# Four slots of split weights, each moved to a different byte offset within 512 bytes

## The reference

```python
proj = jnp.einsum('btd,de->bte', h, w_in[l])            # first block, 2 layers
x = x + jnp.einsum('btd,de->bte', merged, w_out[l])
gu = jnp.einsum('btd,df->btf', h2, w_gate_up[l])
x = x + jnp.einsum('btf,fd->btd', jax.nn.silu(g) * up, w_down[l])
...
proj = h @ w_in[layer]                                   # second block, 1 layer
mix = jnp.concatenate([y_ssd, y_sb], axis=-1) @ w_out[layer]
ffn = (jax.nn.silu(h @ w_gate[layer]) * (h @ w_up[layer])) @ w_down[layer]
```

## Time and profile before

| | |
|---|---|
| median of three runs | 2178.97 us |
| span of the profiled execution | 2177.4 us |
| median less span | 1.6 us |
| TensorE busy | 2165.4 us, 99% |
| GpSimd busy | 1062.6 us, 49% |
| ScalarE busy | 937.9 us, 43% |
| VectorE busy | 1192.0 us, 55% |
| granted TensorE clock over the span | 1.000 |

### The profile page before, as it was taken

One profiled execution on the slowest core, in us unless ns is written; L12 is line 12 of the kernel. 1 busy time (PEld: TensorE's weight loads), 2 busy tenths in 40 slices (PEclk: granted clock), 3 DMA queues, 4 the chain that ended last, 5 costly groups with the idle time before them and its releaser, 6 DMA issues.

```text
span 2177.4 us, 28930 instructions
## 1 busy us (share of the span) xinstructions
PE 2165.4 (99%) x10369; PEld 1750.4 (80%) x10369; DVE 1192.0 (55%) x1584; ACT 937.9 (43%) x1505; POOL 1062.6 (49%) x527
## 2 busy tenths in 40 slices
PE   9999999999999999999999999999999999999999
PEld 7877788888888887788888888887786678888887
DVE  7877854222446887874222335859887746333301
ACT  5556633222214556644333215336645655444311
POOL 4963334444444883244444443433766753444442
PEclk9999999999999999999999999999999999999999
DMA  5332233333662332233333572322221012333332
GB/s 182 105 93 61 69 94 97 96 96 97 214 216 90 107 97 63 68 94 91 96 96 96 183 241 78 107 78 68 68 90 57 30 50 86 106 96 96 96 97 87
DMA packets 62869, 219.57 MB, mean 101 GB/s; under 512 B 7936, under 2 KB 8192, under 8 KB 62784
## 3 DMA queue, kind: packets, MB, share of 16 engines
q1 hardware_dynamic: 55296, 191.16, 28.9%
q10 hardware_dynamic: 7488, 27.27, 3.7%
HBM read 212.76 MB, written 2.10 MB: 99 GB/s over the span
## 4 chain that ended last, share of the span: by engine, by line
PE 93%; DVE 3%; POOL 2%; ACT 1%; issue 1%; DMA 0%; SPq 0%; POOLq 0%; DVEq 0%; ACTq 0%
PE bank L1727 28%; PE bank L1729 28%; PE bank L1728 28%; PE bank L1907 1%; PE bank L1933 1%; PE bank L1967 1%; POOL soft_lo L499 1%; PE bank L1801 1%; DVE soft_hi L1620 1%; POOL wl L408 0%; PE bank L1941 0%; PE bank L2220 0%; DMA raw<-stream 0%; DVE bank L1032 0%; DVE tmp L1621 0%
## 5 line engine op out<-in xcount | busy, mean ns | idle before, releaser
L408 POOL TENSOR_TENSOR wl<-raw,wh 128x1024 fp32r<-128x1024 f32 x349 | 855.1, 2451 | 1003.5 <-ACT wh L555 1003.5
L1727 PE MATMUL bank<-hh,wh 128*128 128x512 f32 (+1 forms) x1979 | 772.7, 390 | 0.9 <-DVE hl L1427 0.6
L1729 PE MATMUL bank<-hh,wl 128*128 128x512 f32 (+1 forms) x1979 | 763.6, 386 | 0.0
L1728 PE MATMUL bank<-hl,wh 128*128 128x512 f32 (+1 forms) x1979 | 763.0, 386 | 0.0
L555 ACT ACTIVATE wh<-raw 128x1024 fp32r<-128x1024 f32 x351 | 370.0, 1055 | 587.2 <-PE bank L1729 537.1
L1727 PEld LDWEIGHTS bank<-hh,wh 128*128 128x128 f32 x1979 | 372.1, 188 | 77.4 <-issue 3.7
L1729 PEld LDWEIGHTS bank<-hh,wl 128*128 128x128 f32 x1979 | 371.9, 188 | 75.5
L1728 PEld LDWEIGHTS bank<-hl,wh 128*128 128x128 f32 x1979 | 372.3, 188 | 73.6 <-issue 1.7
L1729 PE MATMUL bank<-ah,wl 128*128 (+1 forms) x512 | 199.4, 389 | 0.0
L1728 PE MATMUL bank<-al,wh 128*128 (+1 forms) x512 | 199.4, 389 | 0.0
L1727 PE MATMUL bank<-ah,wh 128*128 (+1 forms) x512 | 199.4, 389 | 0.0
(11 more groups left out here) (383 smaller groups left out, 2750.1 us busy)
## 6 DMA issues: line engine op xcount, KB each, us to landing
raw<-stream SPq DMA_DIRECT2D x351, 512.0 KB, 3.6
ada_w<-ada ACTq DMA_DIRECT2D x48, 512.0 KB, 4.6
x<-x_t ACTq DMA_DIRECT2D x4, 512.0 KB, 8.0
out_t<-x SPq DMA_DIRECT2D x8, 256.0 KB, 2.1
th<-q SPq DMA_DIRECT2D x16, 64.0 KB
th<-q SPq DMA_DIRECT2D x64, 16.0 KB
q<-th SPq DMA_DIRECT2D x16, 64.0 KB, 2.0
cst<-consts SPq DMA_DIRECT2D x1, 640.0 KB, 6.8
```

The costliest lines, as they stand in the source:

```text
L408: nc.gpsimd.tensor_tensor(wl[:, slot, :], raw[:, raw_slot, :], wh[:, slot, :].bitcast(F32), ALU.subtract).then_inc(lo_ready, 1)
L1727: mm(dst, wh[:, slot, w], xh, start=start, stop=False)
L1728: mm(dst, wh[:, slot, w], xl, start=False, stop=False)
L1729: return mm(dst, wl[:, slot, w], xh, start=False, stop=stop)
```

## The change

Each slot of wh is made 16 bytes longer than its contents, each slot of wl 96 bytes, and an unused tile of 64 bytes follows. With wh still at byte 57344, the slots of wh start at rests of 0, 16, 32 and 48 by 512. wl starts 64 bytes later than before, and its slots at rests of 64, 160, 256 and 352. The 64 + 384 + 64 bytes that are added make 512, so every tile behind them starts 512 bytes later and at the rest that it had. No instruction is added, removed or moved; only the addresses in `raw -> wh` (L555), `raw, wh -> wl` (L408, L1055) and in the weight loads of L1727 to L1729, L1820 to L1828, L2052 to L2054 and L2088 to L2092 differ.

```diff
-        wh, wl = sb("wh", [P, RW, D], F32R), sb("wl", [P, RW, D], F32R)
+        wh = sb("wh", [P, RW, D + 4], F32R)[:, :, 0:D]
+        wl = sb("wl", [P, RW, D + 24], F32R)[:, :, 0:D]
+        sb("line_up_behind", [P, 16])
         tmp = sb("tmp", [P, 6, T])
```

## The result

The changed kernel takes 2222.66 us (four runs, 2222.46 to 2223.99) against 2178.98 us (2178.60 to 2179.22): 2.0% longer, ratio 1.0200 with an interval of 1.0187 to 1.0212. The profiled execution has a span of 2220.9 us, 43.5 us more than before, with the same number of instructions on each engine.

The account below looks back on a forecast made before the run. TensorE was taken as the bound, matmuls times pitch. Four terms (engines 0, short matmuls folded in, long matmuls' pitch +25 us, tiles behind 0) gave 2177.4 + 25 = 2202 us span, 2204 us median; 8-in-10 range 2145 to 2230 us.

Parts of the forecast that it names:

- What bounds the kernel: Whole kernel: TensorE busy 99%, last chain 93% TensorE; time is number of matmuls times pitch, no new idle time.
- The pitch depends on where load and stream stand to each other: Long matmuls: displacing weights from inputs raises the settled pitch by 3.3 ns, +25 us; chance of pitch going up 0.47.
- The 13.3 ns: Matmuls: most a short one could change either way; if all of it went on the long ones, -113 us.
- The second term: The 273 short matmuls of 256 columns: at most 13.3 ns each either way, 4 us, folded into the long matmuls' pitch.
- the bound of -113 us: Long matmuls, bound from below on their pitch change: all of the 13.3 ns go.
- the third term: Pitch of the long matmuls: 3.3 ns more on 7,400 settled ones, +25 us, bounded by -113 and +41 us.
- The signs: Profile after: 15 feed-forward pitches in 3.45 us instead of 3.40, differing by slot; about 236 matmuls per 54 us, not 240.
- ScalarE and GpSimd at shifted addresses: First term, rounding and subtraction at shifted addresses: taken as 0, with +9 us kept as upper bound.
- everything behind the weights: Fourth term: tiles behind the weights start 512 bytes later at the same rest, costing 0.
- the rival that the subtraction slows: GpSimd's subtraction in the tap stages takes longer, +9 us from above, 2188 us; chance 0.03.
- The rival that addresses do not matter: Pitch stays 226.7 ns in all four slots, 2179 us; chance 0.28.
- The rival that rest 0 is a bad place: Long matmuls: rest 0 was not the best place, so some slots' pitches lie under 226.7 ns; chance 0.22.

Follow-up runs that it names:

- All at 256: All eight weight slots of wh and wl at a rest of 256 from the inputs, against the kernel before: 2179.20 us, ratio 1.0000.
- all at 16: All eight weight slots of wh and wl at a rest of 16 from the inputs, against the kernel before: 2220.11 us, ratio 1.0163.

## Why the prediction was right, and where it was not

The time, 2222.66 us, lies in the range of 2145 to 2230 us and on the side that was forecast. It is 18.7 us beyond the 2204 us named. That the range holds it is in part luck: the dearest pitch that the prediction could bound, +41 us, ends at 2220 us, and the other 9 us of the range's upper end were for a GpSimd that did not slow.

*What bounds the kernel.* Right. The chain stayed at 93% TensorE, and the loss is pitch times number: 39.9 us of the 43.5 lie in the 326 stretches of 24 matmuls in a row. TensorE was to have no new idle time; it has the 2.4 us of two waits in attention, which the sum had no term for.

*The pitch depends on where load and stream stand to each other.* Right for their addresses, and now tested by moving either one: weights alone (+43.7 us with the change), inputs alone (+15.9 us), both together (nothing). How the two stand to each other in time no trace shows. The records of the loads do not help: the earlier trace rows have 188 ns for 128 columns and 137 ns for 64, but the same trace has loads of 128 columns at 141 ns:

```profile
L1967 PEld LDWEIGHTS bank<-cst,prob 128*128 128x128 f32 x128 | 13.7, 141 | 11.2 <-issue 9.1 <-DVE prob L1195 1.5
```

So the length of a load's record does not follow its columns, and how much of it is reading no row shows.

*The 13.3 ns.* The second term (4 us) and the bound of -113 us are made of them, and they are what the third term calls extra cycles. They are an estimate: 226.7 ns less 512 times the 0.417 ns per column by which the earlier trace rows differ. No run shows them as a part of a matmul, nor that they can go: the lowest pitch at which a tile of 512 columns settles is 226.7 ns in every placement. In their place the runs have 0.19 us less on the short matmuls of the changed kernel, with stretches of 117 ns beside the 120.0 ns before, and on the long ones 5.7 ns more in the mean of the four slots.

*The signs.* 15 pitches of about 3.45 us were named and 3.46 to 3.50 came (by the tiles' means); 236 matmuls in 54 us, and 234 came; slots 0 and 3 were to differ, and take 5540 and 5599 ns. A load's record stayed at 188 to 189 ns in the mean of each line.

*The size of the third term.* This is the step that was off. It took the mean of ten pitches behind a disturbance, 3.3 ns, as the nearest row; the four slots of the change have 4.2, 6.5, 5.5 and 6.6 ns over 226.7, 5.7 in the mean. On the 7,400 settled matmuls that is 42 us, not 25. The ten pitches of the earlier trace rows are a mean over a way that leads back to the settled state; the first six, 5.0 ns, were nearer (231, 232, 236, 227, 233 and 231 ns in the trace, and 226 to 228 from the seventh on), but they too were a row of passing pitches, and even the bound of +41 us made from them was a little low.

*Why it stays unsettled.* The prediction had it that the rest changes at every third load, which keeps the pair displaced. That this is needed is refuted: with all loads of a slot alike, at 64, 128 or 384 bytes, no tile settles (5595, 5572 and 5589 ns). Nor is it enough: wh at 16 with wl at 0 changes at every third load too, and settles in all three feed-forwards. What the traces show is that without displacement a stretch comes back to 226.7 ns (313 of 316), and that displacement puts other standing pitches beside that one (16 bytes) or leaves only others (the changed kernel). Why one distance does the first and another the second is open.

*"By 512".* The chosen measure was too coarse. All at 256 is the kernel before to within 0.01 us over the 326 stretches.

*ScalarE and GpSimd at shifted addresses, and everything behind the weights.* The two engines were priced at 0, and their medians moved by 1 and 5 ns; the rival that the subtraction slows has no ground. Moving everything together cost nothing either (all tiles 64 bytes later, ratio 1.0001).

*The rival that addresses do not matter.* Fallen. With the same loads and the same streams, a tile's 5440 ns become 5600 ns by 16 bytes of layout (all at 16). Whether it is read bandwidth that is lost, no run here shows.

*The rival that rest 0 is a bad place.* Fallen as far as it was looked at: of 0, 4, 8, 16, 32, 64, 96, 128, 160, 192, 208, 224, 240, 248 and 252 by 256, none gave a tile below 5440 ns (to 1 ns of rounding).

What stays open is the cause below this. That the loss needs a weight load and a stream side by side was not tried with the load taken away, since each of these matmuls brings its own (the page counts 10369 of both). In all runs `raw` moved with the inputs, so a displacement from `raw`, at which ScalarE and GpSimd read and write, was not separated by an experiment; against it stands that the pitches repeat alike through a whole tile of 5.6 us, while GpSimd works on a chunk for 2.4 us of it and ScalarE for 1.1. What in the chip the displacement acts on, and why 252 settles in the feed-forward and 248 does not, no run here shows.

## What to carry to other kernels

A matmul loop that is bound by TensorE can carry a cost that no engine row shows (TensorE is busy 99% here at a pitch of 226.7 and of 232.35 ns alike): look at the distance from start to start, compare it with the columns it streams, and see whether it repeats. If it does, note the weights' and the inputs' addresses by 256 before anything in front of them is resized, because a change that moves one and not the other cost up to 2.1% here without touching an instruction (nothing where the move was 256 bytes). When a placement is judged, read tiles behind a disturbance as well as the long even stretches, for a layout can be settled in one and not in the other (wh at 16 and wl at 0: 5440 ns in the feed-forwards, 5 us lost elsewhere), and take several executions, for one layout can give two times (2209 and 2221 us with all at 16).

## What the runs showed that was not expected

- One layout can have several standing states. With wh at 16 and wl at 0 they are 226.7, 228.9 and 233.3 ns, and with all at 16 226.7 and 233.3. The runs of these kernels spread too: 2182.55 to 2189.15 us there, and two groups 11 us apart with all at 16, while the changed kernel's four runs lie within 1.6 us.
- The best state is 226.7 ns for 512 columns, in every placement that settles. Single pitches in these traces go down to 223 ns and, waits aside, up to 242 ns, but no tile of 24 with 512 columns took less than 5440 ns, to 1 ns of rounding.
- Matmuls of 256 columns are not hurt: their 267 pitches in a row add up to 0.19 us less than before. After the change the timeline has stretches of 117 ns (the row pair below is 15 pitches apart, 1.76 us) beside the 120.0 ns of the earlier trace rows, so at this length the kernel before did not have the shortest pitch:

```profile
1377.93 0.28 PE L1731 MATMUL bank<-hh,wl 128*128 128x256 f32 x1
...
1379.69 0.28 PE L1731 MATMUL bank<-hh,wl 128*128 128x256 f32 x1
```
